# VectorE's long operations of the first block written as pieces of 512 to 1024 columns

## The reference

```python
h = rmsnorm(x, g_mix[l])
dq, dk, dv, c_q, c_kv_kr, xq, gate_logits = split(h @ w_in[l])
y_diff = diff_attention(dq, dk, dv, ...) @ w_diff_o[l]     # rmsnorm of heads, rotary, causal attention, rmsnorm of outputs
y_mla = latent_attention(c_q, c_kv_kr, ...) @ w_mla_o[l]   # low rank; rotary, rmsnorm of heads of 96
y_mem = memory_cross_attention(xq, mem_n, ...) @ w_cross_o[l]
gates = sigmoid(gate_logits + b_gate[l])                   # three gates of width 1024
x = x + (gates[0] * y_diff + gates[1] * y_mla + gates[2] * y_mem) @ w_out[l]
u = rmsnorm(x, g_mlp[l]) @ w_mlp1[l]                       # width 4096
x = x + square(relu(u)) @ w_mlp2[l]
```

## Time and profile before

| | |
|---|---|
| time, median of 3 runs | 2712.58 us (2710.21 to 2712.6) |
| the profiled execution | 2709.99 us, of it the span of the trace 2708.2 us |
| TensorE busy | 2583.2 us (95%) |
| GpSimd busy | 1920.6 us (71%) |
| VectorE busy | 1087.1 us (40%), 1685 instructions |
| ScalarE busy | 790.1 us (29%) |
| TensorE's granted clock, mean | 0.99 |

### The profile page before, as it was taken

One profiled execution on the slowest core, in us unless ns is written; L12 is line 12 of the kernel. 1 busy time (PEld: TensorE's weight loads), 2 busy tenths in 40 slices (PEclk: granted clock), 3 DMA queues, 4 the chain that ended last, 5 costly groups with the idle time before them and its releaser, 6 DMA issues. The chain is left out here.

```text
span 2708.2 us, 35355 instructions
## 1 busy us (share of the span) xinstructions
PE 2583.2 (95%) x13524; PEld 2083.2 (77%) x13524; DVE 1087.1 (40%) x1685; ACT 790.1 (29%) x1554; POOL 1920.6 (71%) x1599
## 2 busy tenths in 40 slices
PE   7999899999999999999899999999998999989988
PEld 5888567877878887888667878888887976688756
DVE  5544773102221012555674211210102299526884
ACT  4343573000220212242484110120111143523353
POOL 6658606888898898748803888898897779157752
PEclk9999999999999999999999999999999998999989
DMA  5323102333333333422201333333332431043301
GB/s 155 93 57 84 43 1 59 97 93 93 106 91 96 94 97 114 99 65 73 71 1 36 90 93 94 90 97 95 97 97 78 108 81 52 20 97 90 94 4 71
DMA packets 159272, 214.48 MB, mean 79 GB/s; under 512 B 51712, under 2 KB 69376, under 8 KB 159104
## 3 DMA queue, kind: packets, MB, share of 16 engines
q1 hardware_dynamic: 126672, 208.54, 26.9%
q10 hardware_dynamic: 32432, 3.68, 1.1%
HBM read 210.06 MB, written 2.10 MB: 78 GB/s over the span
## 5 line engine op out<-in xcount | busy, mean ns | idle before, releaser
L395 POOL TENSOR_TENSOR weight_parts<-weight_ring,weight_parts 128x512 fp32r<-128x512 f32 (+3 forms) x804 | 1060.8, 1320 | 264.4 <-ACT weight_parts L403 208.9
L392 POOL TENSOR_TENSOR weight_parts<-weight_ring,zero 128x512 fp32r<-128x512 f32 (+3 forms) x702 | 763.9, 1088 | 506.9 <-PE ps L483 342.2
L483 PE MATMUL ps<-h_feature_major_high,weight_parts 128*128 128x512 f32 x2304 | 587.1, 393 | 9.8 <-POOL weight_parts L392 9.5
L483 PEld LDWEIGHTS ps<-h_feature_major_high,weight_parts 128*128 128x128 f32 x2304 | 427.0, 188 | 115.6 <-POOL weight_parts L392 16.8
L481 PE MATMUL ps<-weight_parts,h_feature_major_high 128*128 128x512 f32 (+3 forms) x1904 | 430.0, 363 | 23.3 <-POOL weight_parts L392 10.1
L481 PEld LDWEIGHTS ps<-weight_parts,h_feature_major_high 128*128 128x128 f32 x1904 | 332.6, 189 | 77.9 <-POOL weight_parts L392 15.3
L483 PE MATMUL ps<-h_feature_major_low,weight_parts 128*128 128x512 f32 x1152 | 308.3, 389 | 0.0
L481 PE MATMUL ps<-weight_parts,ut_high 128*128 128x512 f32 x1008 | 251.6, 390 | 1.1 <-POOL weight_parts L392 0.9
L483 PEld LDWEIGHTS ps<-h_feature_major_low,weight_parts 128*128 128x128 f32 x1152 | 216.2, 188 | 45.8
L481 PE MATMUL ps<-weight_parts,h_feature_major_low 128*128 128x512 f32 (+3 forms) x952 | 226.9, 360 | 0.0
L481 PEld LDWEIGHTS ps<-weight_parts,ut_high 128*128 128x128 f32 x1008 | 188.3, 188 | 43.7 <-POOL weight_parts L395 2.2
(11 more groups left out here) (307 smaller groups left out, 3057.8 us busy)
## 6 DMA issues: line engine op xcount, KB each, us to landing
weight_ring<-in_w_in SPq DMA_DIRECT2D x272, 256.0 KB, 2.7
weight_ring<-in_w_mlp SPq DMA_DIRECT2D x256, 256.0 KB, 2.6
weight_ring<-in_w_out SPq DMA_DIRECT2D x64, 256.0 KB, 2.6
weight_ring<-in_w_mem_kv SPq DMA_DIRECT2D x32, 256.0 KB, 2.9
weight_ring<-in_w_diff_o SPq DMA_DIRECT2D x32, 256.0 KB, 2.7
weight_ring<-in_w_in SPq DMA_DIRECT2D x32, 170.0 KB, 2.3
weight_ring<-in_w_in SPq DMA_DIRECT2D x32, 168.0 KB, 2.2
weight_ring<-in_w_in SPq DMA_DIRECT2D x32, 163.0 KB, 2.2
```

The lines of the kernel that those rows point to most:

```text
L392: self.nc.gpsimd.tensor_tensor(high, raw, self.m["zero"][:].broadcast_to([P, raw.shape[1]]), ALU.add).then_inc(self.s["slab_high"], 1)
L395: self.nc.gpsimd.tensor_tensor(low, raw, high.bitcast(F32), ALU.subtract).then_inc(self.s["slab_split"], 1)
L483: last = self.nc.tensor.matmul(banks[:, t, :], w[:, cut], h, **ends)
```

## The change

Each of the operations named above that reads two operands in SBUF and is longer than 1024 columns is written as two or four operations, by token tile or by chunk, on the same data, and the semaphore is signalled by the last one. L1513 (1024 columns) and L1688 stay as they are. By columns: L1514, L1554, L1691, L1697, L1718 from 2048 to 4 x 512; L1631 from 1536 to 2 x 768; L1677 from 4096 to 4 x 1024.

```diff
@@ -1511,7 +1511,9 @@
             v.drain()
             mkv, xqv = (b.rearrange("p t (h d) -> p t h d", h=CH) for b in (mk, xq))
             v.tensor_tensor(mkv, mkv, bc(st_mk, [P, 2, CH, CHD], 3), ALU.mult)
-            v.tensor_tensor(xqv, xqv, bc(st_xq, [P, TT, CH, CHD], 3), ALU.mult).then_inc(s["cross_normed"], 1)
+            for t in range(TT):
+                last = v.tensor_tensor(xqv[:, t], xqv[:, t], bc(st_xq[:, t, :], [P, CH, CHD], 2), ALU.mult)
+            last.then_inc(s["cross_normed"], 1)
             dve.wait_ge(s["lam_exps"], 1)
             v.tensor_tensor(lam_neg, dots[:, 1:2], dots[:, 0:1], ALU.subtract)
             v.drain()
@@ -1551,7 +1553,8 @@
                     v.tensor_tensor(y1, y1, turns[0], ALU.subtract)
                     v.tensor_tensor(y2, y2, turns[1], ALU.add)
                     v.drain()
-                    v.tensor_tensor(dst, dst, bc(stat, [P, TT, 8, DHD], 3), ALU.mult)
+                    for t in range(TT):
+                        v.tensor_tensor(dst[:, t], dst[:, t], bc(stat[:, t, :], [P, 8, DHD], 2), ALU.mult)
                     v.drain()
 
                 return products, sums
@@ -1628,7 +1631,8 @@
 
             def square_mla(t, which):
                 (src, st), squared = both[which], squared_of[which]
-                v.tensor_tensor(squared, src[:, t:t + 2], src[:, t:t + 2], ALU.mult)
+                for k in range(2):
+                    v.tensor_tensor(squared[:, k], src[:, t + k], src[:, t + k], ALU.mult)
                 v.drain()
                 v.tensor_reduce(st[:, t:t + 2, :], squared, AX.X, ALU.add)
                 v.drain()
@@ -1673,8 +1677,10 @@
             v.drain()
 
             rstd(st_o, [(st_o, P)])
-            odv = od.rearrange("p t (h d) -> p (t h) d", h=DH)
-            v.tensor_tensor(odv, odv, bc(st_o.rearrange("p t h -> p (t h)"), [P, TT * DH, P], 2), ALU.mult).then_inc(s["outs_ready"], 1)
+            for t in range(TT):
+                odv = od[:, t, :].rearrange("p (h d) -> p h d", h=DH)
+                last = v.tensor_tensor(odv, odv, bc(st_o[:, t, :], [P, DH, P], 2), ALU.mult)
+            last.then_inc(s["outs_ready"], 1)
             for name in merge_order:
                 if name[0] == "o":
                     L.write_low(name, split[name])
@@ -1688,14 +1694,18 @@
                     v.tensor_tensor(merging if b == 0 else gated, L.banks(name), g, ALU.mult).then_inc(s["dve_emptied"], 1)
                     if b:
                         v.drain()
-                        last = v.tensor_tensor(merging, merging, gated, ALU.add)
+                        for j in range(4):
+                            last = v.tensor_tensor(merging[:, j, :], merging[:, j, :], gated[:, j, :], ALU.add)
                         if b == 1:
                             v.drain()
                     if b == 2:
                         last.then_inc(s["merging_done"], 1)
                         dve.wait_ge(s["merged_high"], half + 1)
-                        v.tensor_tensor(mrg[1][:, 4 * half:4 * half + 4, :], merging, mrg[0][:, 4 * half:4 * half + 4, :].bitcast(F32),
-                                        ALU.subtract).then_inc(s["merged"], 1)
+                        for j in range(4):
+                            c = 4 * half + j
+                            last = v.tensor_tensor(mrg[1][:, c, :], merging[:, j, :], mrg[0][:, c, :].bitcast(F32),
+                                                   ALU.subtract)
+                        last.then_inc(s["merged"], 1)
 
             L.add_left(dve, "wo0", hn)
             for high, low, src, gain in left:
@@ -1715,8 +1725,10 @@
                 for j in range(ups):
                     L.highs += 1
                     dve.wait_ge(s["high_written"], L.highs)
-                    v.tensor_tensor(ut[1][:, 4 * j:4 * j + 4, :], rect[(f * ups + j) % 2], ut[0][:, 4 * j:4 * j + 4, :].bitcast(F32),
-                                    ALU.subtract).then_inc(s["dve_emptied"], 1)
+                    for c in range(4):
+                        last = v.tensor_tensor(ut[1][:, 4 * j + c, :], rect[(f * ups + j) % 2][:, c, :],
+                                               ut[0][:, 4 * j + c, :].bitcast(F32), ALU.subtract)
+                    last.then_inc(s["dve_emptied"], 1)
                 if layer == f == 0:
                     dve.wait_ge(s["next_mem_loaded"], 16)
                     for t in range(2):
```

## The result

The changed kernel takes 2699.34 us (median of 5 runs, 2697.04 to 2701.94), the one before 2712.58 (5 runs, 2710.21 to 2712.73). The ratio is 0.9949, 95% interval 0.9937 to 0.996: faster by 13 us, where 16.4 were predicted. The profiled execution has a span of 2695.9 us against 2708.2.

The account below looks back on a forecast made before the run. TensorE, busy 95%, bounds the kernel; it waits for GpSimd, held out by long VectorE instructions. Gains of 12.8 us a layer less a 4.6 us merge stall give 8.2, 16.4 in both: 2696 us, range 2686 to 2706.

Parts of the forecast that it names:

- The mechanism: Between two VectorE pieces GpSimd gets one instruction in; 512 columns hold its high part up 0.45 us, its low part 0.33.
- Rival 2: Consecutive pieces keep GpSimd out like one instruction, so the change does nothing: 2712.6 us, chance 0.07.
- rival 4: At the merge's end each piece waits for both parts of a slab, 3.1 us a piece: 2719 us, chance 0.04.
- The merge's stall: End of the merge: wo0's chunk 4 waits for the later subtraction, 4.6 us a layer (3.6 to 5.6).
- rival 1: The stall at the merge's end doesn't come, as pieces run back to back: 2687.0 us, chance 0.16.
- rival 3: The stalls also bring TensorE 7 us at half clock, up to 3.4 us once a layer: 2703.0 us, chance 0.11.
- L1514: 2048 columns to 4 x 512: the TensorE stall behind it goes, gain 0.9 us a layer.
- L1691 with L1697: The merge's four adds and two subtractions in pieces: no delay exceeds GpSimd's lead, gain 5.8 us a layer.
- L1677: 4096 columns to 4 x 1024: TensorE loses 2.6 us now, 1.2 stay, gain 1.4 us a layer.
- L1554: Four times 2048 columns to 4 x 512: gain 0, at worst some tenths of a us either way.
- L1631: Four squares of 1536 columns to 2 x 768, where GpSimd is behind: gain 1.7 us a layer (0.5 to 2.5).
- L1718: Eight subtractions a layer, 2048 columns to 4 x 512: 0.40 us or a little less each, gain 3.0 us a layer.

Follow-up runs that it names:

- the last experiment: L1677 in eight pieces of 512 columns instead of four of 1024, against the changed kernel with TensorE waiting for the merge by chunk: 2687.4 us, ratio 0.9903.

## Why the prediction was right, step by step

The time fell into the range, 3 us above the forecast. By its steps:

- **The mechanism** was right: one instruction of GpSimd gets in between two pieces, and 512 columns hold it up by 0.45 or 0.33. The rows show 1.46 to 1.49 and 1.62 us beside pieces of 512 where GpSimd has work ready. Beside pieces of 768 and 1024 they show 1.76 and 1.89, 2.02 and 2.16, as predicted too. Rival 2 falls with this, and with it rival 4: a piece takes about 1.5 us, not 3.1.
- **The merge's stall** was right to 0.1 us (4.48 for 4.6), so rival 1 falls. **What stands behind the stall** was the step that failed: the forecast took 4.6 us as its whole price, and rival 3, that it costs clock too, had 0.11. Rival 3 came about together with the forecast. The clock was down for 6.8 us from within each of the two waits, and the stretch cost 7.3 and 7.5 us instead of 4.6. That is 5.6 us of the time. Eight kernels without the stall, the one before among them, in which the clock stays up in wo0, and three others with it, in which it falls in both layers, show it.
- **L1514, L1691 with L1697, L1677:** 0.75 and 0.4 us for 0.9, 5.6 for 5.8, 1.2 for 1.4. L1554, put at nothing or some tenths, brings 0.4. The 1.2 us that "stay" behind pieces of 1024 are right as well, by the last experiment.
- **L1631:** predicted 1.7 (0.5 to 2.5), and 1.5 measured at the slab that the prediction looked at. Its list was right slab by slab: without the 1.2 us gained ahead of it, the changed kernel's slabs start at 274.6, 277.6, 281.2, 284.3, 287.3 and 291.0, for 274.5, 277.5, 281.2, 284.3, 287.2 and 290.9. The step stopped there; the attention comes next, and there TensorE gave 0.8 and 1.0 back and kept 0.7 and 0.5. How this divides between L1091 beside L813 and the clock is open.
- **L1718:** mis-sized, 3.9 and 3.3 us for 3.0. Each costs 0.41. In layer 0 alone the fourth is followed at once by L1445, which squares the next layer's memory in two operations of 1024 columns and holds GpSimd up as well (L392 takes 2.02 us beside it, L395 2.15). The whole L1718's hold-up of 1.93 comes on top of these, that of the pieces less; the rows fit this, and no run tests it.
- **Small delays of VectorE** that were called covered were covered: in TensorE's list of waits there is no new one for VectorE but L1706.
- **The sum:** 2 x 8.2 predicted; the first block shows 10.7 in the profiled executions (5.3 and 5.5), and the medians differ by 13.2. That the forecast was only 3 us off is in part luck: the clock behind the stalls took 5.6 us, and L1718 (1.2), L1554 (0.8) and the second block's variation gave some of it back. The excess of the medians is within what the second block varies by itself.

A single large tile pays SBUF's latency once and many small ones pay it each (the Trainium skill, "VectorE: DVE Perf Modes", section "The TRN2 errata — SBUF-src ops pay a fixed extra latency per instruction"). The prediction cites this under "SBUF — State Buffer", where it doesn't stand. The fixed part is there, but here it is 0.16 us a piece on an engine that is busy 45% of the time. By that rule alone the merge's add would have grown from 2.29 to 2.8 us; it took 5.29, because the pieces also let GpSimd's instructions in between. And the 128 instructions more, which the rule speaks against, go with a kernel that is 0.5% faster.

## What to carry to other kernels

If two engines hold each other out, the length of one's instruction matters by what it takes from the other's lead in one go. Cut it to where the supplier can regain one hold-up before the next has used up its lead (512 columns here; for L1718 1024 gave nearly nothing). Cut operations end later, because the other engine now gets its turns: look for whoever waits for the last piece, and let it wait for the first instead, as one signal by chunk turned a loss of 7.4 us a layer into 0.3. And price a stall of TensorE with the clock behind it, not by its own length.

## What the runs showed that I had not expected

- A single wait of 4.5 us put TensorE's granted clock to 0.50 and cost 2.8 to 3.0 us beyond itself in the changed kernel. Over all traces the clock fell in each of the eight places where it stood, for 1.7 to 3.0 us. The wait of 2.35 us did it in four places of eight, for some 1.6 us. It didn't in the kernel before, from which the prediction concluded that nothing like it is seen there. Waits of 1.4 us at the merge did not.
- Two pieces of 1024 columns cost TensorE almost what one of 2048 costs (0.34 beside 0.40), while four of 512 cost nothing.
- Twelve traces of kernels with an identical second block differ there by up to 7.7 us, with the clock low in different places. Edits worth under 2 us a layer show in the matmuls' starts only, not in the medians.
